# Three weight units taken together behind a norm, the third from a place of its own, in a two-block transformer kernel

## The chip, the cores and the metric

The kernel runs on one core of a Trainium2 chip. A time is the device microseconds of one execution, and the figure for the kernel is the median of its runs. One further execution was taken with the hardware profiler; its span, from the first instruction to the last, is what the rows below come from.

## The reference

The input is one sequence of 256 tokens of 1024 numbers. It goes through one mixer block with a feed-forward part, and then through two hybrid layers, each again with a feed-forward part. All of it is in float32. What matters here is the order of normalizations and matrix products:

```python
h = rms_norm(x, norm_mix_g[l]);  proj = h @ w_in[l]        # "win1"
...
x = x + merged @ w_out[l]                                  # "wout1"
h = rms_norm(x, norm_ffn_g[l])                             # norm "ffn"
u = causal_dwconv(h @ ffn_up[l], ...)                      # "up1"
x = x + (gelu(u_gate) * u_val) @ ffn_down[l]               # "down1"
x = rms_norm(x, final_norm_g)                              # norm "final"
# two layers, l = 0, 1:
proj = einsum('bsd,de->bse', x, w_in)                      # "win20", "win21"
...
x = layer_norm(ALPHA * x + mix, ln1_g, ln1_b)              # "wout2l", norm "ln1l"
up = causal_dwconv_2(einsum('bsd,df->bsf', x, w_up), ...)  # "up20", "up21"
x = layer_norm(ALPHA * x + ffn, ln2_g, ln2_b)              # "down2l", norm "ln2l"
```

Each norm needs sums over all 1024 numbers of a token, so nothing of the product behind it can start before the last tile in front of it is finished.

## The kernel before, in words

**Layout.** Numbers of a token lie on the partitions, tokens along the free dimension: x is eight tiles of 128x256 (KT = 8). Every weight matrix is cut into units of eight 128x128 blocks (seven in part of the down products). There are 400 units, in the order of `unit_table`; `START[name]` is the number of the first unit of a phase (up1 88, win20 156, up20 210, win21 278, up21 332).

**Precision.** Each operand is split into a high and a low part in a rounded float32 format, and each block product is three matmuls of 256 columns: high by high, high by low, low by high (`product_of`, lines 1097 to 1103). A unit of eight blocks is 24 matmuls into one PSUM bank. The unit's last matmul increments `unit_done`.

**The ring of three.** A unit goes through four steps on four queues, with three slots (RING = 3) of each of `raw`, `whi`, `wlo`; unit n has slot n % 3:

- SyncE issues the load into `raw` (`load`, L522). It waits until the low part of unit n - 3 is made (`split_lo`).
- ScalarE copies `raw` into `whi` (`hi_part`, L766). It waits for the load and until TensorE has done unit n - 3.
- VectorE subtracts: `wlo = raw - whi` (`lo_part`, L1400). It waits for `split_hi` of the unit.
- TensorE waits for `split_lo` of the unit (`begin`, line 1105).

So the split of unit n + 3 begins when unit n is finished, and runs beside units n + 1 and n + 2. In a phase, ScalarE first takes the result of unit n out of its bank (L1046, L1044 in up, L1079 in win2), and then makes the high part of unit n + 3; in up, VectorE does the two convolution taps of unit n (L1712, L1715) ahead of the low part.

**Behind a norm.** VectorE makes the normalized tiles (L1419 for an rms norm, L1440 for a layer norm), ScalarE their high parts (L810, L800), VectorE their low parts (L1404, L1444; two of eight on GpSimd after an rms norm, L702). TensorE follows tile by tile in `ramp` (lines 1125 to 1140): by `TOGETHER` it takes block k of the first two units of the phase as soon as normalized tile k is there, 6 matmuls for each k, 48 in all. The third unit follows by `plain`, and so do all others. Between the tiles in front of the norm and the ramp, TensorE does the sums over the partitions and small filler matmuls (`warm`, L1117).

**The third unit before.** Its `whi` slot is that of the last unit in front of the norm. Its high part is made on ScalarE behind the sums: after `norm_inverse` in an rms norm, between tiles 2 and 3 in a layer norm (`norm_shift`, line 794). Its low part is made on VectorE after all normalized tiles: in `up` by the body of i = 0, in win2 by a call ahead of the loop (line 1755).

Of the kernel before, what the change touches and what calls it, by code (L numbers as in the profile page):

```python
# [80 lines left out]
UNITS, START = unit_table()  # L81
FFNS = ("1", "20", "21")


# [120 lines left out]
def build(nc, args, out):  # L205
# [3 lines left out]
    with ctx:  # L209
# [63 lines left out]
        var_rows, mean_rows = fprod[:, 0, :], fprod[:, 2, :]  # L273
        shift_rows = acc[:, 0, :]
        pads = sb("pads", [P, 4, 2, 16 + S])
        zpad = sb("zpad", [P, 2, 2 + S])
# [77 lines left out]
        def repeat(eng, name, count, per, body, peel_first=False):  # L354

            rounds = count // per
            lo, hi = (1 if peel_first else 0), rounds - 1
            n0 = START[name]  # L360
            for i in range(lo * per):
                body(n0 + i, i, 0)
            if hi > lo:
                with eng.Fori(lo, hi) as it:
                    for i in range(per):
                        body(n0 + i, i, it)
            for i in range(hi * per, count):
                body(n0 + i, i, 0)

        def head(j):  # L370
# [75 lines left out]
        def bank_of(r):  # L446
            return unit_bank[r % 3]
# [310 lines left out]
        def _(act):  # L758
            def hi_part(n, it=0, per=0):
                if n >= len(UNITS):  # L760
                    return
                blocks = UNITS[n][3]

                wait(act, arrived[n % RING], 16 * (n // RING + 1), it, 16 * per // RING)
                wait(act, unit_done, n - RING + 1, it, per)
                act.activation(whi[:, n % RING, 0:blocks * P], raw[:, n % RING, 0:blocks * P], ACT.Copy).then_inc(split_hi, 1)  # L766

# [25 lines left out]

            def norm_shift(which, last, third=None):

                for t in range(KT):
                    if t == 3 and third is not None:
                        hi_part(third)
                    act.wait_ge(scaled, KT * LNI[which] + t + 1)
                    act.activation(x[:, t, :] if last else xhi[t], dev[:, t, :], ACT.Identity, bias=col(which[:3] + "_b" + which[3], t)) \  # L800
                        .then_inc(normed_act if last else x_hi, 1)
                    if t == 3 and which in NEXT:
                        shift_copy(NEXT[which])
# [197 lines left out]
            def wout(first, which, begun=0):  # L1001
                for t in range(KT):
                    if t >= begun:
                        hi_part(first + t + 2)
                    if t == 0:
                        load_log()
                    if t:
                        square(which, t - 1)
                square(which, KT - 1)

            def down(name, which):
                def body(n, i, it):
# [12 lines left out]
                repeat(act, name, DOWN, 6, body, peel_first=True)  # L1025
                if which not in LNI:
                    square(which, KT - 2)
                square(which, KT - 1)

# [30 lines left out]
            norm_inverse("ffn", RMS_EPS)  # L1060
            hi_part(START["up1"] + 2)
            norm_hi("ffn", dev)
            ffn(0, "up1", "ffn_1", False)
            down("down1", "final")
            norm_inverse("final", RMS_EPS)
            hi_part(START["win20"] + 2)
            norm_hi("final", x)

            for l in range(LAYERS2):
# [18 lines left out]
                norm_inverse(f"ln1{l}", LN_EPS)  # L1088
                norm_shift(f"ln1{l}", False, START[f"up2{l}"] + 2)
# [3 lines left out]
                norm_shift(f"ln2{l}", l == LAYERS2 - 1, START[f"win2{l + 1}"] + 2 if l < LAYERS2 - 1 else None)  # L1093


        @block.tensor
        def _(pe):
            def product_of(ps, slot, block, hi, lo, first, last):

                w = slice(block * P, (block + 1) * P)  # L1100
                pe.matmul(ps, whi[:, slot, w], hi, start=first, stop=False)  # L1101
                pe.matmul(ps, whi[:, slot, w], lo, start=False, stop=False)  # L1102
                return pe.matmul(ps, wlo[:, slot, w], hi, start=False, stop=last)  # L1103

# [16 lines left out]

            TOGETHER = [(u, k) for k in range(KT) for u in range(2)]
            LATER = [(u, k) for u in range(2) for k in range(5)] + TOGETHER[10:]

            def ramp(n, result, ready, order=TOGETHER, split=(xhi, xlo), shift=False):

                hi, lo = split
                met = [0, 0]
                for u, k in order:
                    if k == 0:  # L1130
                        begin(n + u, result + u)
                    if k == max(met):
                        pe.wait_ge(*ready[k])
                    met[u] = k + 1
                    mm = product_of(bank_of(result + u)[:, 0:S], (n + u) % RING, k, hi[k], lo[k], k == 0, k == KT - 1)
                    if k == KT - 1:
                        mm.then_inc(unit_done, 1)
                    if shift and (u, k) == (1, 0):
                        pe.matmul(shift_sum, ones_hi[:], hi[0], start=True, stop=True).then_inc(shift_ready, 1)

            def plain(n, result, ps, it=0, per=0, rper=0, ready=None, split=(xhi, xlo)):
                hi, lo = split
                begin(n, result, it, per, rper)
                for k in range(KT):
                    if ready is not None:
                        pe.wait_ge(*ready[k])
                    mm = product_of(ps, n % RING, k, hi[k], lo[k], k == 0, k == KT - 1)
                mm.then_inc(unit_done, 1)
# [146 lines left out]
            def merge_unit(n, r, t, parts, ready):  # L1295
# [6 lines left out]
                for which, (y, blocks) in enumerate(parts):  # L1302
                    ps = branch_bank(r, which, t)
                    for k in range(blocks):
                        mm = product_of(ps, n % RING, b, yhi[y + k], ylo[y + k], k == 0, k == blocks - 1)
                        b += 1
# [17 lines left out]
            def up(name, which):  # L1324
                def body(n, i, it):
                    r = RESULT[name] + i
                    if i < 2 and isinstance(it, int):
                        if i == 0:
                            ramp(n, r, lows(which), shift=which in NEXT)
                        return  # L1330
# [3 lines left out]
            def down(name, f, which):  # L1334
                def body(n, i, it):
# [5 lines left out]
                    if i in (2, 4) and isinstance(it, int) and it == 0:  # L1341
                        product_of(ps_turn[:, 0:S], n % RING, 0, xhi[0], xlo[0], True, True)
                    for k in range(DOWN_PARTS[part]):
                        mm = product_of(down_bank(name, t)[:, 0:S], n % RING, k, fhi[:, k0 + k, :], flo[:, k0 + k, :],
                                        k0 + k == 0, k0 + k == FT - 1)
# [20 lines left out]
            for l in range(LAYERS2):  # L1366
                name = f"win2{l}"
                ramp(START[name], RESULT[name], lows("ln20" if l else "final"), shift=True)
                for p, (kind, t) in enumerate(PLAN2):
                    n, r = START[name] + p, RESULT[name] + p  # L1370
                    if kind == "merge":
                        merge_unit(n, r, t, [(0, 2), (2, 4), (6, 2)],
                                   [(out_read, 8 + 4 * (l + 1)), (pool_lo, l + 1), (gconv_lo, 2 * l + 2)])
                    elif p > 1:
                        plain(n, r, bank_of(r)[:, 0:S])
# [9 lines left out]
        def _(dve):  # L1385
# [8 lines left out]
            def lo_part(n, it=0, per=0):  # L1394
                if n >= len(UNITS):
# [3 lines left out]
                wait(dve, split_hi, n + 1, it, per)  # L1399
                dve.tensor_tensor(wlo[:, n % RING, w], raw[:, n % RING, w], whi[:, n % RING, w].bitcast(f32), ALU.subtract) \  # L1400
                    .then_inc(split_lo, 1)
# [295 lines left out]
            def wout(name, which, alpha, begun=0):  # L1697
                for t in range(KT):
                    if t >= begun:
                        lo_part(START[name] + t + 2)  # L1700
                    if t == 0 and which in LNI:
                        dve.wait_ge(x_shifted, KT * (LNI[which] + 1))
                    residual(name, t, START[name] + t, alpha, bank_of(RESULT[name] + t), which)

            def up(f, name, cols, width):
                def body(n, i, it):
                    lo_part(n + 2, it, 6)
                    q = KT + UPT * f + i
# [10 lines left out]
            def down(name, which, alpha):  # L1719
                def body(n, i, it):  # L1720
# [11 lines left out]
                    if i % 3 == 2:  # L1732
                        residual(name, t, n, alpha, down_bank(name, t), which, it, 6, 2)
                repeat(dve, name, DOWN, 6, body, peel_first=True)

            for n in range(WIN1):
# [150 lines left out]
```

## Time and profile before

| | us |
|---|---|
| median of three runs | 1200.94 (1200.78 to 1202.69) |
| the profiled execution's own time | 1200.8 |
| its span | 1199.0 |
| TensorE busy in it | 1181.3 |
| VectorE busy | 849.5 |
| ScalarE busy | 713.8 |
| GpSimd busy | 441.5 |

The mean granted clock of TensorE is 0.998 of 2.4 GHz. A busy share of TensorE is counted from the modelled ends of pipelined matmuls: a matmul of 256 columns has a row of 0.28 us, and the next begins 0.11 to 0.12 us after it. A pause of TensorE shows therefore in the distance between the starts of matmuls rather than in its busy time. In the timeline a row is: start in us, duration in us, engine, line, operation, output<-inputs, sizes, how many in a row were merged, and in brackets how long the engine had been idle and what ended that.

### The profile page before, as it was taken

To read this page: it belongs to the slowest core of one execution; us is meant where nothing else is said; L and a number is where in the kernel's file an instruction comes from. 1 tells how busy PE (TensorE), PEld (TensorE's weight loads), DVE (VectorE), ACT (ScalarE), POOL (GpSimd) and SP (SyncE) were. 2 spreads that over 40 slices of the span, in tenths; PEclk is the share of its full clock that TensorE was granted. 3 is DMA by queue.
4 is the path that set the end of the run, shared out by engine and by line. 5 is a ranking of instruction groups with operands and counts; after the bars stand their busy time and mean duration, and the time that the engine had idled before them with its cause. 6 is when DMAs were issued, how large, how long until landed. Compare 5 with 4: busy or idle time off the path is not lost.

```text
span 1199.0 us, 27004 instructions
## 1 busy us (share of the span) xinstructions
PE 1181.3 (99%) x10128; PEld 1160.6 (97%) x10128; DVE 849.5 (71%) x1399; ACT 713.8 (60%) x1242; POOL 441.5 (37%) x415
## 2 busy tenths in 40 slices
PE   8999999999999999999999999999999999999997
PEld 7999999999999999999999999999999999999996
DVE  5868665676877764878667877755877677877754
ACT  5767667545766654566456666645566456666643
POOL 3007315123344402232338534423622349444422
PEclk9999999999999999999999999999999999999999
DMA  7554445654655666454554655566544554665563
GB/s 260 184 165 159 132 157 164 192 192 159 194 192 192 188 189 197 158 161 147 181 189 140 203 189 193 179 196 182 160 162 155 188 173 151 201 197 191 180 201 100
DMA packets 60286, 212.61 MB, mean 177 GB/s; under 512 B 6688, under 2 KB 7968, under 8 KB 60064
## 3 DMA queue, kind: packets, MB, share of 16 engines
q1 hardware_dynamic: 60192, 211.32, 55.9%
q8 instruction: 64, 1.05, 0.4%
q14 instruction: 30, 0.25, 0.1%
HBM read 210.24 MB, written 1.05 MB: 176 GB/s over the span
## 4 chain that ended last, share of the span: by engine, by line
PE 89%; DVE 5%; issue 2%; ACT 2%; POOL 1%; POOLq 0%; DVEq 0%; ACTq 0%
PE bank L1101 28%; PE bank L1103 28%; PE bank L1102 28%; DVE wlo L1400 2%; PE bank L1117 1%; PE bank L1249 1%; PE bank L1218 1%; ACT whi L766 1%; PE bank L1229 1%; PE bank L1273 1%; DVE prob L1565 1%; DVE prob L1540 0%; POOL u L683 0%; DVE u L1632 0%; PE bank L1158 0%
## 5 line engine op out<-in xcount | busy, mean ns | idle before, releaser
L1400 DVE TENSOR_TENSOR wlo<-raw,whi 128x1024 fp32r<-128x1024 f32 (+1 forms) x400 | 499.9, 1250 | 204.2 <-ACT whi L766 202.5
L1101 PE MATMUL bank<-shifted,whi 128*128 128x256 f32 x2296 | 639.0, 278 | 1.5 <-POOL shifted L702 1.1
L1102 PE MATMUL bank<-shifted,whi 128*128 128x256 f32 x2296 | 636.2, 277 | 0.0
L1103 PE MATMUL bank<-shifted,wlo 128*128 128x256 f32 x2296 | 635.8, 277 | 0.0
L766 ACT ACTIVATE whi<-raw 128x1024 fp32r<-128x1024 f32 (+1 forms) x400 | 416.5, 1042 | 149.4 <-PE bank L1103 137.9
L1101 PEld LDWEIGHTS bank<-shifted,whi 128*128 128x128 f32 x2296 | 431.6, 188 | 3.4 <-POOL shifted L702 1.3
L1103 PEld LDWEIGHTS bank<-shifted,wlo 128*128 128x128 f32 x2296 | 431.7, 188 | 0.0
L1102 PEld LDWEIGHTS bank<-shifted,whi 128*128 128x128 f32 x2296 | 431.1, 188 | 0.0
L662 POOL TENSOR_TENSOR fprod<-ugate,uval 128x256 f32<-128x256 f32 x66 | 95.5, 1447 | 197.5 <-DVE uval L1715 188.2
L1101 PE MATMUL bank<-fhi,whi 128*128 128x256 f32 x528 | 145.8, 276 | 0.0
L1102 PE MATMUL bank<-flo,whi 128*128 128x256 f32 x528 | 145.7, 276 | 0.0
L1103 PE MATMUL bank<-fhi,wlo 128*128 128x256 f32 x528 | 145.7, 276 | 0.0
L1101 PE MATMUL bank<-aligned,whi 128*128 128x256 f32 x334 | 101.7, 305 | 3.4 <-DVE aligned L1404 3.4
L683 POOL TENSOR_TENSOR u<-u,tmp 128x256 f32<-128x256 f32 x48 | 53.4, 1112 | 134.2 <-DVE tmp L1674 132.2
L1101 PEld LDWEIGHTS bank<-fhi,whi 128*128 128x128 f32 x528 | 99.1, 188 | 0.0
L1102 PEld LDWEIGHTS bank<-flo,whi 128*128 128x128 f32 x528 | 99.1, 188 | 0.0
L1103 PEld LDWEIGHTS bank<-fhi,wlo 128*128 128x128 f32 x528 | 99.1, 188 | 0.0
L1103 PE MATMUL bank<-aligned,wlo 128*128 128x256 f32 x334 | 93.2, 279 | 0.0
L1102 PE MATMUL bank<-aligned,whi 128*128 128x256 f32 x334 | 92.3, 276 | 0.0
L1101 PEld LDWEIGHTS bank<-aligned,whi 128*128 128x128 f32 x334 | 62.8, 188 | 12.0 <-issue 9.1
L696 POOL TENSOR_TENSOR acc<-acc,dev 128x256 f32<-128x256 f32 x34 | 36.4, 1069 | 82.9 <-DVE dev L1694 51.8
L1102 PEld LDWEIGHTS bank<-aligned,whi 128*128 128x128 f32 x334 | 62.9, 188 | 0.4
(218 smaller groups left out, 1258.7 us busy)
## 6 DMA issues: line engine op xcount, KB each, us to landing
raw<-in_w_win SPq DMA_DIRECT2D x140, 512.0 KB, 3.5
raw<-in_w_up SPq DMA_DIRECT2D x132, 512.0 KB, 3.5
raw<-in_w_down SPq DMA_DIRECT2D x48, 448.0 KB, 3.5
raw<-in_w_merge SPq DMA_DIRECT2D x32, 512.0 KB, 3.6
raw<-in_w_out SPq DMA_DIRECT2D x24, 512.0 KB, 4.3
raw<-in_w_down SPq DMA_DIRECT2D x24, 512.0 KB, 3.5
x<-in_x SPq DMA_DIRECT2D x4, 256.0 KB, 4.5
rgw<-in_rg_w SPq DMA_DIRECT2D x1, 1024.0 KB, 10.1
```

What stands on the lines that cost most here:

```text
L662: pool.tensor_tensor(tile(fprod, t % 3), tile(ugate, t % 3), tile(uval, t % 3), ALU.mult).then_inc(product, 1)
L683: ins = pool.tensor_tensor(m, m, branch_part(base, t, branch), ALU.add)
L696: pool.tensor_tensor(acc[:, sums, :], acc[:, sums, :], one, ALU.add).then_inc(done, 1)
L766: act.activation(whi[:, n % RING, 0:blocks * P], raw[:, n % RING, 0:blocks * P], ACT.Copy).then_inc(split_hi, 1)
L1101: pe.matmul(ps, whi[:, slot, w], hi, start=first, stop=False)
L1102: pe.matmul(ps, whi[:, slot, w], lo, start=False, stop=False)
L1103: return pe.matmul(ps, wlo[:, slot, w], hi, start=False, stop=last)
L1117: pe.matmul(bank_of(result)[:, S:S + P], ones[:], ones[:], start=True, stop=True)
L1218: mm = pe.matmul(score_bank(j)[:, rows:rows + across], u[qp:qp + HD, q, rows:cols], u[kp:kp + HD, k, 0:across], start=True, stop=True, ski ...
L1229: mm = pe.transpose(ps_turn[:, i * P:(i + 1) * P], prob[:, s, i * P:(i + 1) * P], ident)
L1249: mm = pe.matmul(ps_out[m * i:m * i + m, half * P:S], v[:, half, c:c + m], probT[:, job % 2, half * S:half * P + S], start=half == 0, stop ...
L1400: dve.tensor_tensor(wlo[:, n % RING, w], raw[:, n % RING, w], whi[:, n % RING, w].bitcast(f32), ALU.subtract) \
```

## The change

The third unit of the five phases up1, win20, up20, win21 and up21 (units 90, 158, 212, 280, 334) gets a place of its own for its high and low part, `third`. The place lies where `pads` and `zpad` lie, which only the win2 phases use, at other times. Its high part no longer waits for the last unit in front of the norm, but for the one before that; ScalarE makes it ahead of the last square in front of the sums, and VectorE makes its low part right after the last residual. The parts made behind the sums go. TensorE takes the three units together by the order `THREE`: for k = 0, 1, 2 blocks of the first two units; for k = 3 to 7 block k of the first two and block k - 3 of the third; then blocks 5, 6, 7 of the third. The first unit then ends with matmul 57 of 72 (before: 45), the second with matmul 60 (before: 48), the third with matmul 72 (before: 72). The waits of all other units are as they were.

```diff
+THIRD = [START[name] + 2 for name in ("up1", "win20", "up20", "win21", "up21")]
...
+        with ExitStack() as three:
+            sb("line_third", [P, 16], stack=three)
+            third = sb("third", [P, 2, 8 * P], r32, stack=three)
         pads = sb("pads", [P, 4, 2, 16 + S])
...
+        def high_part(n, it=0):
+            return third[:, 0, :] if n in THIRD and isinstance(it, int) else whi[:, n % RING, :]
+        def low_part_of(n, it=0):
+            return third[:, 1, :] if n in THIRD and isinstance(it, int) else wlo[:, n % RING, :]
...
                 wait(act, arrived[n % RING], 16 * (n // RING + 1), it, 16 * per // RING)
-                wait(act, unit_done, n - RING + 1, it, per)
-                act.activation(whi[:, n % RING, 0:blocks * P], raw[:, n % RING, 0:blocks * P], ACT.Copy).then_inc(split_hi, 1)
+                wait(act, unit_done, n - RING + (0 if n in THIRD and isinstance(it, int) else 1), it, per)
+                act.activation(high_part(n, it)[:, 0:blocks * P], raw[:, n % RING, 0:blocks * P], ACT.Copy).then_inc(split_hi, 1)
...
-            def norm_shift(which, last, third=None):
+            def norm_shift(which, last):
                 for t in range(KT):
-                    if t == 3 and third is not None:
-                        hi_part(third)
...
             def wout(first, which, begun=0):
...
                         square(which, t - 1)
+                hi_part(first + KT + 2)
                 square(which, KT - 1)
             def down(name, which):
...
                     square(which, KT - 2)
+                hi_part(START[name] + DOWN + 2)
                 square(which, KT - 1)
...
             norm_inverse("ffn", RMS_EPS)
-            hi_part(START["up1"] + 2)
...
             norm_inverse("final", RMS_EPS)
-            hi_part(START["win20"] + 2)
...
             TOGETHER = [(u, k) for k in range(KT) for u in range(2)]
+            THREE = [(u, k - 3 * (u == 2)) for k in range(KT + 3) for u in range(3) if 0 <= k - 3 * (u == 2) < KT]
...
-                met = [0, 0]
+                met = [0, 0, 0]
...
-                    if i < 2 and isinstance(it, int):
+                    if i < 3 and isinstance(it, int):
                         if i == 0:
-                            ramp(n, r, lows(which), shift=which in NEXT)
+                            ramp(n, r, lows(which), THREE, shift=which in NEXT)
...
-                ramp(START[name], RESULT[name], lows("ln20" if l else "final"), shift=True)
+                ramp(START[name], RESULT[name], lows("ln20" if l else "final"), THREE, shift=True)
...
-                    elif p > 1:
+                    elif p > 2:
                         plain(n, r, bank_of(r)[:, 0:S])
...
                     residual(name, t, START[name] + t, alpha, bank_of(RESULT[name] + t), which)
+                lo_part(START[name] + KT + 2)
             def up(f, name, cols, width):
                 def body(n, i, it):
-                    lo_part(n + 2, it, 6)
+                    if i or not isinstance(it, int):
+                        lo_part(n + 2, it, 6)
...
                 repeat(dve, name, DOWN, 6, body, peel_first=True)
+                lo_part(START[name] + DOWN + 2)
...
-                lo_part(START[f"win2{l}"] + 2)
```

The products read their weight parts through `high_part` and `low_part_of` in place of the slot.

## Rows read from the trace of the kernel before

**Rows 1.** Page: busy us, share of the span, instructions; shares of the chain by engine

```profile
PE 1181.3 (99%) x10128; PEld 1160.6 (97%) x10128; DVE 849.5 (71%) x1399; ACT 713.8 (60%) x1242; POOL 441.5 (37%) x415
...
PE 89%; DVE 5%; issue 2%; ACT 2%; POOL 1%; POOLq 0%; DVEq 0%; ACTq 0%
```

**Rows 2.** Timeline, TensorE behind the first FFN norm: start us, us, engine line op

```profile
297.68 0.32 PE L1101 MATMUL bank<-shifted,whi 128*128 128x256 f32 x1
...
300.89 0.28 PE L1101 MATMUL bank<-shifted,whi 128*128 128x256 f32 x1
...
304.00 0.31 PE L1101 MATMUL bank<-aligned,whi 128*128 128x256 f32 x1
```

**Rows 3.** Timeline, ScalarE and VectorE in the same stretch (engine columns as above)

```profile
299.48 1.21 DVE L1400 TENSOR_TENSOR wlo<-raw,whi 128x1024 fp32r<-128x1024 f32 x1
...
301.10 0.56 ACT L1046 ACTIVATE ugate<-bank,vec 128x256 f32<-128x256 f32 x1 [2.31 <-PE bank L1103]
...
301.56 1.05 ACT L766 ACTIVATE whi<-raw 128x1024 fp32r<-128x1024 f32 x1
...
302.21 0.48 DVE L1715 SCALAR_TENSOR_TENSOR ugate<-bank,vec,ugate 128x254 f32<-128x254 f32 x1
...
302.65 1.23 DVE L1400 TENSOR_TENSOR wlo<-raw,whi 128x1024 fp32r<-128x1024 f32 x1
```

**Rows 4.** Timeline, TensorE, ScalarE, VectorE behind the norm into up20

```profile
652.70 0.36 PE L1101 MATMUL bank<-shifted,whi 128*128 128x256 f32 x1
...
656.35 0.47 ACT L1044 ACTIVATE ugate<-bank,vec 128x256 f32<-128x256 f32 x1 [2.00 <-PE bank L1103]
...
657.28 0.28 PE L1101 MATMUL bank<-shifted,whi 128*128 128x256 f32 x1
...
657.80 1.23 DVE L1400 TENSOR_TENSOR wlo<-raw,whi 128x1024 fp32r<-128x1024 f32 x1
...
659.32 0.28 PE L1101 MATMUL bank<-aligned,whi 128*128 128x256 f32 x1
```

**Rows 5.** Timeline, TensorE and ScalarE behind the norm into win20

```profile
484.03 0.28 PE L1101 MATMUL bank<-shifted,whi 128*128 128x256 f32 x1
...
487.41 0.39 ACT L1079 ACTIVATE u<-bank 128x256 f32<-128x256 f32 x1 [2.42 <-PE bank L1103]
...
490.39 0.28 PE L1101 MATMUL bank<-aligned,whi 128*128 128x256 f32 x1
```

**Rows 6.** Timeline, VectorE alone in that stretch

```profile
488.77 1.23 DVE L1400 TENSOR_TENSOR wlo<-raw,whi 128x1024 fp32r<-128x1024 f32 x1 [1.89 <-ACT whi L766]
```

**Rows 7.** Timeline, TensorE and ScalarE behind the norm into win21

```profile
840.14 0.38 PE L1101 MATMUL bank<-shifted,whi 128*128 128x256 f32 x1
...
843.77 0.38 ACT L1079 ACTIVATE u<-bank 128x256 f32<-128x256 f32 x1 [1.97 <-PE bank L1103]
...
846.85 0.28 PE L1101 MATMUL bank<-aligned,whi 128*128 128x256 f32 x1
```

**Rows 8.** Timeline, VectorE alone in that stretch

```profile
845.13 1.23 DVE L1400 TENSOR_TENSOR wlo<-raw,whi 128x1024 fp32r<-128x1024 f32 x1 [1.28 <-ACT whi L766]
```

**Rows 9.** Timeline, around the sums of the first FFN norm

```profile
291.53 0.42 ACT L987 ACTIVATE dev<-x 128x256 f32<-128x256 f32 x1 [1.77 <-DVE x L1694]
...
293.57 1.04 ACT L766 ACTIVATE whi<-raw 128x1024 fp32r<-128x1024 f32 x1
293.67 1.26 DVE L1419 SCALAR_TENSOR_TENSOR dev<-x,vec,bank 128x256 f32<-128x256 f32 x3 [2.17 <-ACT bank L781]
```

**Rows 10.** Timeline, around the sums of the norm into win20

```profile
471.82 3.29 SPq L522 DMA_DIRECT2D raw<-in_w_win  x2
...
477.59 0.42 ACT L987 ACTIVATE dev<-x 128x256 f32<-128x256 f32 x1 [1.41 <-DVE x L1694]
```

**Rows 11.** Timeline, VectorE at the sums of the norm into win21

```profile
834.22 0.42 DVE L1428 TENSOR_TENSOR fprod<-bank,fprod 128x256 f32<-128x256 f32 x1 [1.38 <-PE bank L1187]
```

**Rows 12.** Page: DMA issues, KB each, median us from issue to landing

```profile
raw<-in_w_win SPq DMA_DIRECT2D x140, 512.0 KB, 3.5
```

More of the change, by code:

```diff
@@ L1088, in _ @@
                 norm_inverse(f"ln1{l}", LN_EPS)
-                norm_shift(f"ln1{l}", False, START[f"up2{l}"] + 2)
+                norm_shift(f"ln1{l}", False)
                 ffn(1 + l, f"up2{l}", f"ffn_2{l}", True)
@@ L1092, in _, with product_of @@
                 norm_inverse(f"ln2{l}", LN_EPS)
-                norm_shift(f"ln2{l}", l == LAYERS2 - 1, START[f"win2{l + 1}"] + 2 if l < LAYERS2 - 1 else None)
+                norm_shift(f"ln2{l}", l == LAYERS2 - 1)
         @block.tensor
         def _(pe):
-            def product_of(ps, slot, block, hi, lo, first, last):
+            def product_of(ps, n, it, block, hi, lo, first, last):
                 w = slice(block * P, (block + 1) * P)
-                pe.matmul(ps, whi[:, slot, w], hi, start=first, stop=False)
-                pe.matmul(ps, whi[:, slot, w], lo, start=False, stop=False)
-                return pe.matmul(ps, wlo[:, slot, w], hi, start=False, stop=last)
+                pe.matmul(ps, high_part(n, it)[:, w], hi, start=first, stop=False)
+                pe.matmul(ps, high_part(n, it)[:, w], lo, start=False, stop=False)
+                return pe.matmul(ps, low_part_of(n, it)[:, w], hi, start=False, stop=last)
             def begin(n, result, it=0, per=0, rper=0, banks=3):
@@ L1134, in ramp @@
                     met[u] = k + 1
-                    mm = product_of(bank_of(result + u)[:, 0:S], (n + u) % RING, k, hi[k], lo[k], k == 0, k == KT - 1)
+                    mm = product_of(bank_of(result + u)[:, 0:S], n + u, 0, k, hi[k], lo[k], k == 0, k == KT - 1)
                     if k == KT - 1:
@@ L1146, in plain @@
                         pe.wait_ge(*ready[k])
-                    mm = product_of(ps, n % RING, k, hi[k], lo[k], k == 0, k == KT - 1)
+                    mm = product_of(ps, n, it, k, hi[k], lo[k], k == 0, k == KT - 1)
                 mm.then_inc(unit_done, 1)
@@ L1304, in merge_unit @@
                     for k in range(blocks):
-                        mm = product_of(ps, n % RING, b, yhi[y + k], ylo[y + k], k == 0, k == blocks - 1)
+                        mm = product_of(ps, n, 0, b, yhi[y + k], ylo[y + k], k == 0, k == blocks - 1)
                         b += 1
@@ L1341, in body @@
                     if i in (2, 4) and isinstance(it, int) and it == 0:
-                        product_of(ps_turn[:, 0:S], n % RING, 0, xhi[0], xlo[0], True, True)
+                        product_of(ps_turn[:, 0:S], n, it, 0, xhi[0], xlo[0], True, True)
                     for k in range(DOWN_PARTS[part]):
-                        mm = product_of(down_bank(name, t)[:, 0:S], n % RING, k, fhi[:, k0 + k, :], flo[:, k0 + k, :],
+                        mm = product_of(down_bank(name, t)[:, 0:S], n, it, k, fhi[:, k0 + k, :], flo[:, k0 + k, :],
                                         k0 + k == 0, k0 + k == FT - 1)
@@ L1399, in lo_part @@
                 wait(dve, split_hi, n + 1, it, per)
-                dve.tensor_tensor(wlo[:, n % RING, w], raw[:, n % RING, w], whi[:, n % RING, w].bitcast(f32), ALU.subtract) \
+                dve.tensor_tensor(low_part_of(n, it)[:, w], raw[:, n % RING, w], high_part(n, it)[:, w].bitcast(f32), ALU.subtract) \
                     .then_inc(split_lo, 1)
```

## The prediction

> **What bounds the kernel now.** I read the page first, for the engine that sets the time. TensorE is busy 99% of the span, and the chain of work that ended last lies on it for 89% [rows 1]. So what counts is when TensorE starts each matmul, and a pause of TensorE is lost unless a later pause swallows it. Then I read the timeline behind the five norms that the change touches, and in it the starts of TensorE's matmuls, counted from the first matmul of the ramp (number 0).
>
> Behind the first FFN norm, matmul 18 starts at 297.68, matmul 45 at 300.89, and matmul 72, the first of unit 91, at 304.00 [rows 2]. The 54 matmuls from 18 to 72 take 6.32 us, 0.117 each. Behind the norm into win20 the same 54 take 6.36 us, 0.1178 each [rows 5]. These two are rms norms, and their ramps hold no pause to speak of. Behind the norm into up20, a layer norm, the 54 take 6.62 us, while the last 18 of them (from matmul 54 at 657.28) take 2.04, 0.1133 each [rows 4]. At that pitch 54 would take 6.12, so 0.50 us of pauses lie there: TensorE waits a little for each normalized tile. Into win21 the 54 take 6.71 us [rows 7]; at 0.1178 they would take 6.36, so 0.35 us of pauses. The norm into up21 repeats up20's pattern.
>
> The second thing to see is how the ring is refilled behind the ramp. Unit 91 has the slot of unit 88, and its split starts when unit 88, the first of the ramp, is done. Matmul 44 is unit 88's last. ScalarE takes its result at 301.10, which is 0.21 after matmul 45 has started [rows 2, 3]. It then makes the high part of unit 91 from 301.56. VectorE does two taps, the second at 302.21, and the low part from 302.65 to 303.88 [rows 3]. From ScalarE's start to the end of the low part are 2.78 us. TensorE starts unit 91 at 304.00, 0.12 later [rows 2]. With 0.21 and 0.12 the refill takes 3.11 us from the start of matmul 45, and the 27 matmuls from 45 to 72 take 304.00 - 300.89 = 3.11 us. Unit 91 comes just in time; **there is no slack in this refill**. In up20 the middle part is 656.35 to 659.03, 2.68 us [rows 4]. In the win2 phases, which have no taps, it is 2.59 us: 487.41 to 490.00 [rows 5, 6] and 843.77 to 846.36 [rows 7, 8].
>
> **The change part by part.**
>
> *The order of the ramp.* By the new order unit 88 ends with matmul 57 in place of 45, since the third unit's matmuls are put between. From the start of its successor, matmul 57, only 15 matmuls are left to matmul 72, not 27. The split of the fourth unit still waits for the first one: its wait is not touched, as only the third has a place of its own. So the refill, some 3 us, has 15 x 0.117 = 1.76 us to hide behind. What is queued behind TensorE's wait for the fourth unit's low part is everything that TensorE has left.
>
> I work it out forward from matmul 18, which is the same in both: up to there both orders have the same matmuls. From there TensorE has 9 matmuls for each tile, about 1.03 us, in place of 6, about 0.69. A pause at a tile of at most 0.50/5 us or so goes away by that, so I take the undisturbed pitch. The fourth unit starts at (matmul 18) + 39 x pitch + 0.21 + middle part + 0.12:
>
> - up1: 297.68 + 39 x 0.117 + 0.21 + 2.78 + 0.12 = 305.35, before 304.00: +1.35.
> - win20: 484.03 + 39 x 0.1178 + 0.21 + 2.59 + 0.12 = 491.54, before 490.39: +1.15.
> - up20: 652.70 + 39 x 0.1133 + 0.21 + 2.68 + 0.12 = 660.13, before 659.32: +0.81.
> - win21: 840.14 + 39 x 0.1178 + 0.21 + 2.59 + 0.12 = 847.65, before 846.85: +0.80.
> - up21, as up20: +0.81.
>
> The sum is **+4.92 us**. The layer norms' smaller terms already contain the pauses that the third unit fills. With every pitch at 0.1133 it is 4.92 - 39 x (0.0037 + 2 x 0.0045) = 4.4; with every pitch at 0.1178, 4.92 + 39 x (0.0008 + 2 x 0.0045) = 5.3. The units after the fourth have room again: in up1 the next low part was made about 2 us after this one, and a unit takes 24 x 0.1133 = 2.7 us.
>
> *The high part, moved ahead of the sums.* 1.06 us or so on ScalarE, five times (1.04 us where it stood) [rows 9]. It stands ahead of the last square, which feeds the sums. ScalarE was idle for 1.77 us there in up1 and 1.41 into win20 [rows 9, 10], waiting for TensorE's last tile, so it fits with 0.35 to 0.7 us over, if its load has landed. Into win20 the load was issued at 471.82, as soon as the low part of unit 155 was made, and takes 3.5 us in the median [rows 10, 12], so it lands at about 475.3; ScalarE has until 477.59 - 1.06 = 476.5. I cost it at nothing. If that cover is gone, each us of delay is a us in front of the norm.
>
> *The low part, moved ahead of the norm.* 1.23 us on VectorE, behind the last residual. VectorE's idle time there was 2.17 in up1 and, least of all, 1.38 us into win21 [rows 9, 11]: hidden, by 0.15 us in the tightest place. Behind it are queued the first norm operations. Nothing.
>
> *What goes behind the sums.* The high part at 293.57 delayed the first high part of a normalized tile a little in the rms norms, but VectorE does three scalings first, until 293.67 + 1.26 [rows 9], and reaches the first low part only then. I bound the gain by 0 and 0.1 us in each of two norms and take 0. The low part at 299.48 [rows 3] ran beside the ramp and cost nothing; its going gives nothing.
>
> *The queues of SyncE and GpSimd.* The load that reuses the third unit's `raw` slot waits for its low part, which is now made some 8 us earlier: before at 299.48 [rows 3], now behind the last residual, about when the last square starts at 291.53 [rows 9]. The load goes out earlier; later ones still wait for the splits. GpSimd does nothing for weight parts. Nothing on the path. The place `third` shares its memory with `pads`, with no wait added.
>
> **Sum.** The profiled execution took 1200.8 us (span 1199.0, 1.8 around it), the median 1200.94, so the difference is 0.1. 1200.94 + 4.9 = 1205.8 us.
>
> **Rivals.**
>
> *The third unit fills pauses and nothing is lost* (the other side). TensorE pauses in each layer-norm ramp, and with a third unit ready it need not. The Trainium skill, page Perfetto Trace Analysis, section Optimization Strategy, reads consistent bubbles on the engine that should be saturated as a possible sign that there isn't enough SBUF for the next tile; by that rule another place should shorten the time. The trace agrees that there are bubbles, but they end with the normalized tile and not with a weight part. From rows the gain is 0.50 + 0.35 + 0.50 = 1.35 us, with 0.1 to 0.2 from the rms norms: 1199.4 us. It decides if the refill, from the first unit's end to the fourth unit's low part, takes less than the 15 matmuls, 1.76 us. Against it: the refill took 2.9 to 3.1 us in all four places that I read, and in up1 unit 91 started 0.12 us after its low part ended. Chance 0.04.
>
> *The lost time is swallowed, or the order does not do what it says.* If TensorE waited later for VectorE in the win2 phases whatever it did before, the two win2 terms would go: 4.92 - 1.95 = 2.97, 1203.9 us. I hold this for the forecast's lower end, since VectorE's work there starts from TensorE's results. If the third unit is in truth taken after the first two, all stays: 1200.9 us. Chance of that, or of all five terms being swallowed, 0.05.
>
> *The moved split lands on the sums as well.* If loads land late, or VectorE's low part grows past its 1.38 us in the tight places, the norm starts later on top of the forecast. At most 1.06 us each time, five times, if no cover held: up to 1205.8 + 5.3 = 1211.1 us; half of it, about 1208.5, is likelier. For it speaks only the tightness in two places. Chance 0.08.
>
> **How the numbers follow.** The forecast has the remaining 0.83, and its own range is 1203.9 (win2 terms swallowed) to 1207.0 (highest pitch, and some tenths for the tight places). The chance outside is 0.17, so the range need not reach to the rivals: 1203.9 to 1207.2. Slower by over 0.2% (over 2.4 us, about what a measurement of this kernel can tell from no change) takes the forecast and the third rival, 0.91; within 0.2% 0.05; faster, from the first rival, which with 1.5 us would partly fall within, 0.04.
>
> **What would show it right or wrong.** Right: behind each of the five norms TensorE starts its ramp when it did, has no pause between matmuls 18 and 72, and then pauses 1.2 to 1.4 us before matmul 72's successor unit, with VectorE's low part (L1400 of before) as what ends the wait; the high part of the fourth unit starts about 0.6 us after matmul 57 has. ScalarE's last square and the first scaling stand where they stood against the last matmul in front of the norm. Wrong: no pause at the fourth unit (then the refill found more cover than I count), or an idle gap of TensorE ahead of the ramp that has grown (then the moved split is not hidden), or later pauses of TensorE in win2 that have shrunk by as much.

## The result and the profile after

The changed kernel takes 1206.81 us in the median of 6 runs (1205.35 to 1208.06), the kernel before 1201.45 in 6 runs of the same comparison (1200.78 to 1202.69). The ratio is 1.0042, with a 95% interval of 1.0032 to 1.0052: the change makes the kernel 5.4 us slower, and the time lies 1 us above the forecast, inside the range.

The profiled execution took 1208.06 us, 7.3 more than that of before, and 2.5 of these lie in the first phase, win1, whose code is the same in all nine traces: it takes 210.8 to 210.9 us in five of them and 212.9 to 213.5 in four, this one among them, with a granted clock of 0.50 to 0.54 between 16 and 22 us where the five have 1.00; I therefore compare the other phases from here on, and leave out of the figures below one execution of the kernel "both together" that took 1944.07 us at a mean granted clock of 0.567.

The page of the changed kernel, the rows that answer to [rows 1]:

```profile
span 1206.3 us, 27004 instructions
PE 1183.9 (98%) x10128; PEld 1162.3 (96%) x10128; DVE 847.8 (70%) x1399; ACT 714.9 (59%) x1242; POOL 433.0 (36%) x415
PE 88%; DVE 6%; issue 2%; ACT 2%; POOL 1%; POOLq 0%; DVEq 0%; ACTq 0%
```

TensorE is still what bounds the kernel. The view of TensorE's waits says what is new: what it waited for, us in total, times, longest. First the two largest rows of the kernel before, then the two largest of the changed one:

```profile
PE bank L1101 <- DVE aligned L1404: 3.4, 3, 1.8
PE bank L1117 <- ACT ones_hi L816: 2.5, 1, 2.5
```

```profile
PE bank L1112 <- DVE wlo L1412: 5.1, 5, 1.2
PE bank L1112 <- DVE aligned L1416: 3.2, 3, 1.8
```

Before, no row named a low part. Now five waits, one behind each of the five norms, cost 5.1 us together. (The view counts a wait from the modelled end of the row in front, which is 0.17 us later than the start that the next matmul would have had at the usual distance; by the starts the five waits are 6.0 us.) This is the first of them in the timeline, behind the first FFN norm (start, length, engine; idle time and its releaser in brackets). It answers to [rows 2, 3]:

```profile
299.88 0.31 PE L1112 MATMUL bank<-shifted,whi 128*128 128x256 f32 x1
...
304.36 0.28 PE L1112 MATMUL bank<-shifted,whi 128*128 128x256 f32 x1
...
304.56 0.56 ACT L1059 ACTIVATE ugate<-bank,vec 128x256 f32<-128x256 f32 x1 [3.58 <-PE bank L1114]
...
305.02 1.05 ACT L779 ACTIVATE whi<-raw 128x1024 fp32r<-128x1024 f32 x1
...
305.68 0.48 DVE L1729 SCALAR_TENSOR_TENSOR ugate<-bank,vec,ugate 128x254 f32<-128x254 f32 x1
...
305.95 0.28 PE L1114 MATMUL bank<-shifted,third 128*128 128x256 f32 x1
...
306.11 1.23 DVE L1412 TENSOR_TENSOR wlo<-raw,whi 128x1024 fp32r<-128x1024 f32 x1
...
307.39 0.39 PE L1112 MATMUL bank<-aligned,whi 128*128 128x256 f32 x1 [1.17 <-DVE wlo L1412]
...
307.61 0.28 PE L1113 MATMUL bank<-aligned,whi 128*128 128x256 f32 x1
```

The rows are matmuls 18, 57, 71, 72 and 73 with the refill between them. Matmul 57 follows the first unit's last. ScalarE takes that unit's result 0.20 us later, splits off the high part of the fourth unit at 305.02, VectorE finishes the low part at 307.34, and TensorE goes on at 307.39: 3.03 us, of which only the matmuls 57 to 71, until about 306.06, lie beside it. Compare [rows 2]: the same refill lay beside 27 matmuls, and nothing stood still. The other four waits:

```profile
494.93 0.39 PE L1112 MATMUL bank<-aligned,whi 128*128 128x256 f32 x1 [0.91 <-DVE wlo L1412]
...
664.60 0.39 PE L1112 MATMUL bank<-aligned,whi 128*128 128x256 f32 x1 [1.07 <-DVE wlo L1412]
...
852.94 0.38 PE L1112 MATMUL bank<-aligned,whi 128*128 128x256 f32 x1 [0.98 <-DVE wlo L1412]
...
1022.98 0.39 PE L1112 MATMUL bank<-aligned,whi 128*128 128x256 f32 x1 [1.01 <-DVE wlo L1412]
```

The five phases behind the norms (up1, win20, up20, win21, up21, each from its first matmul to that of the next phase) take 650.54 us, 5.25 more than the 645.29 of before. The two rms ramps start 0.11 us earlier each, which shortens wout1 and down1. The remaining phases agree within 0.1 us. Net, that is 5.03 us.

The moved splits are seen around the sums, in front of the first FFN norm, the rows that answer to [rows 9]:

```profile
292.05 1.06 ACT L779 ACTIVATE third<-raw 128x1024 fp32r<-128x1024 f32 x1
...
293.72 1.22 DVE L1412 TENSOR_TENSOR third<-raw,third 128x1024 fp32r<-128x1024 f32 x1
...
293.83 0.42 ACT L998 ACTIVATE dev<-x 128x256 f32<-128x256 f32 x1 [0.72 <-DVE x L1706]
...
295.97 1.26 DVE L1431 SCALAR_TENSOR_TENSOR dev<-x,vec,bank 128x256 f32<-128x256 f32 x3 [1.03 <-ACT bank L794]
```

ScalarE's idle time ahead of the last square fell from 1.77 to 0.72 us, and VectorE's ahead of the first scaling from 2.17 to 1.03. Both splits went into idle time, with something left over.

### The profile page after: what moved, and what is told of

Read it like the earlier page. It is cut to its first block, busy times and chain, and to the rows that moved or that the text cites. A ratio compares the mean times of both kernels' runs of the same rounds, so it can differ in the third digit from the quotient of the medians.

```text
span 1206.3 us, 27004 instructions
## 1 busy us (share of the span) xinstructions
PE 1183.9 (98%) x10128; PEld 1162.3 (96%) x10128; DVE 847.8 (70%) x1399; ACT 714.9 (59%) x1242; POOL 433.0 (36%) x415
## 4 chain that ended last, share of the span: by engine, by line
PE 88%; DVE 6%; issue 2%; ACT 2%; POOL 1%; POOLq 0%; DVEq 0%; ACTq 0%
PE bank L1112 28%; PE bank L1114 27%; PE bank L1113 27%; DVE wlo L1412 2%; PE bank L1128 1%; PE bank L1261 1%; PE bank L1230 1%; ACT whi L779 1%; PE bank L1241 1%; PE bank L1285 1%; DVE prob L1577 1%; DVE prob L1552 0%; POOL u L696 0%; DVE u L1644 0%; PE bank L1170 0%
## 5 line engine op out<-in xcount | busy, mean ns | idle before, releaser
L1412 DVE TENSOR_TENSOR wlo<-raw,whi 128x1024 fp32r<-128x1024 f32 (+1 forms) x395 | 492.0, 1247 | 213.1 <-ACT whi L779 211.2
L1112 PE MATMUL bank<-shifted,whi 128*128 128x256 f32 x2261 | 629.7, 279 | 1.3 <-POOL shifted L715 0.9
L1113 PE MATMUL bank<-shifted,whi 128*128 128x256 f32 x2261 | 627.5, 278 | 0.0
L1114 PE MATMUL bank<-shifted,wlo 128*128 128x256 f32 x2261 | 627.2, 277 | 0.0
L779 ACT ACTIVATE whi<-raw 128x1024 fp32r<-128x1024 f32 (+1 forms) x395 | 411.5, 1042 | 151.6 <-PE bank L1114 135.6
L1112 PEld LDWEIGHTS bank<-shifted,whi 128*128 128x128 f32 x2261 | 426.0, 188 | 2.9 <-POOL shifted L715 1.2
L1114 PEld LDWEIGHTS bank<-shifted,wlo 128*128 128x128 f32 x2261 | 426.2, 189 | 0.0
L1113 PEld LDWEIGHTS bank<-shifted,whi 128*128 128x128 f32 x2261 | 425.5, 188 | 0.0
```

The costliest lines, as they stand in the source:

```text
L779: act.activation(high_part(n, it)[:, 0:blocks * P], raw[:, n % RING, 0:blocks * P], ACT.Copy).then_inc(split_hi, 1)
L1112: pe.matmul(ps, high_part(n, it)[:, w], hi, start=first, stop=False)
L1113: pe.matmul(ps, high_part(n, it)[:, w], lo, start=False, stop=False)
L1114: return pe.matmul(ps, low_part_of(n, it)[:, w], hi, start=False, stop=last)
L1412: dve.tensor_tensor(low_part_of(n, it)[:, w], raw[:, n % RING, w], high_part(n, it)[:, w].bitcast(f32), ALU.subtract) \
```

## The experiments

Two theories at the start. **The order** costs the time: the first unit ends at matmul 57, the refill of its slot has 15 matmuls to hide behind, and TensorE waits for the rest. The rival: **the moved splits or the own place** cost it, by what they delay at the sums or on VectorE. Each kernel is the changed one with the edit shown. The times are medians, each beside the kernel before on the same chip: 1202.32 us (27 runs) for the kernels lag and four, 1202.18 (23 runs) for first, first_four and filled.

### The lag of the third unit: 8, 5 and 0 tiles

The third unit follows the first two by 3 normalized tiles in the change. One number sets it:

```diff
-THREE = [(u, k - 3 * (u == 2)) for k in range(KT + 3) for u in range(3) if 0 <= k - 3 * (u == 2) < KT]
+THREE = [(u, k - 8 * (u == 2)) for k in range(KT + 8) for u in range(3) if 0 <= k - 8 * (u == 2) < KT]
```

and the same with 5 and with 0. With 8 the third unit comes behind the first two, as before the change, while its place and the moved splits stay. The first unit's successor is then matmul 45, with a lag of 5 it is 51, with 3 it is 57, with 0 it is 66.

Lag 8:

> The changed kernel with the third unit's 24 matmuls moved behind the other two units (a lag of 8 tiles in place of 3). Its own place and the moved splits stay. Theory 1 (the refill of the fourth unit lies open because the first unit ends 12 matmuls later): the first unit ends with matmul 45 again, 27 matmuls cover the refill of 2.8 to 3.0 us, no wait for a low part behind any ramp, the small pauses of the layer-norm ramps come back; time 1200.5 to 1201.5 us, the kernel before's. Rival (the splits moved ahead of the sums, or the new place, cost the time): stays at 1205 us or more.

Measured: 1202.0 us (11 runs), ratio 0.9998 (0.9989 to 1.0007). Lag 5:

> The changed kernel with a lag of 5 tiles in place of 3. The first unit ends with matmul 51, so 21 matmuls (2.4 us) are left for the refill of 2.8 to 3.0 us. Theory 1: a wait of 0.3 to 0.6 us behind each of the five ramps, in all +2.0 us against the kernel before, 1203 us. Rival (the interleaving as such, or the moved splits, cost the time): as the change, 1205.5 us.

Measured: 1203.51 us (11 runs), ratio 1.0021 (1.0012 to 1.0030). Lag 0:

> The changed kernel with no lag: the three units side by side from the first tile. The first unit ends with matmul 66, 6 matmuls (0.7 us) are left. Theory 1: a wait of about 2.2 us behind each ramp, 1 us more than in the change, partly paid back in the layer-norm ramps where the third unit fills two more small pauses; in all +9.5 us against the kernel before, 1210.5 us. Rival (interleaving as such): 1205 to 1206 us. Rival (the third unit fills pauses): faster than the change.

Measured: 1214.89 us (4 runs), ratio 1.0115 (1.0099 to 1.0131). TensorE's waits for the low part, in lag 5 first, then in lag 0; lag 8 has no such row:

```profile
PE bank L1112 <- DVE wlo L1412: 1.8, 5, 0.5
```

```profile
PE bank L1112 <- DVE wlo L1412: 10.4, 5, 2.2
```

The distance from matmul 71 to 72, from the timelines (0.11 us is no wait):

| lag | matmuls left | up1 | win20 | up20 | win21 | up21 | five phases against before |
|---|---|---|---|---|---|---|---|
| 8 | 27 | 0.11 | 0.11 | 0.11 | 0.11 | 0.11 | -0.90 |
| 5 | 21 | 0.76 | 0.48 | 0.67 | 0.62 | 0.67 | +2.85 |
| 3 (the change) | 15 | 1.44 | 1.19 | 1.35 | 1.26 | 1.29 | +5.25 |
| 0 | 6 | 2.46 | 2.27 | 2.37 | 2.35 | 2.37 | +12.62 |

From lag 5 to 3, six matmuls go from behind the first unit to ahead of its end, 6 x 0.1136 = 0.68 us; the wait grows by 0.62 to 0.71. From 3 to 0 nine go, 1.02 us; it grows by 1.02 to 1.09. **The wait is the refill less the matmuls left, and the order is the whole loss.** The rival is out: lag 8 has the own place and both moved splits, and loses nothing.

Lag 0 lost 12.6 us against the kernel before where I had forecast 9.5, and not by its waits. (Its 1214.89 us is 4.4 above the 1210.5 of the forecast; the other 1.3 is the kernel before, at 1202.32 here.) In the profiled execution, TensorE's granted clock fell behind two of the five waits, in up1 and win21. This is the table by stretch in up1 (us, busy time and instructions of PE, PEld, DVE, ACT and POOL, granted clock, DMA share, GB/s): in front of the wait, around it, the first matmuls of the fourth unit, the rest of that unit, and the next one. The last two rows are the rest of the fourth unit in win21, and the whole fourth unit in up20, where the clock stayed.

```profile
303.00:306.00 3.00, 3.00 (x29) 3.00 (x27) 0.00 (x0) 0.45 (x1) 0.00 (x0) 1.00 0.00 0
306.00:308.38 2.38, 0.20 (x3) 0.00 (x1) 2.19 (x4) 2.38 (x4) 0.00 (x0) 1.00 0.00 0
308.38:309.40 1.02, 1.02 (x8) 1.02 (x9) 0.98 (x3) 1.00 (x2) 0.00 (x0) 0.96 0.00 0
309.40:312.60 3.20, 3.20 (x17) 3.20 (x16) 2.85 (x4) 2.49 (x5) 0.73 (x1) 0.50 0.82 224
312.83:316.00 3.17, 3.17 (x29) 3.17 (x28) 2.16 (x4) 1.96 (x4) 1.01 (x1) 1.00 0.68 238
...
859.20:862.40 3.20, 3.20 (x17) 3.20 (x16) 2.52 (x6) 0.04 (x1) 0.47 (x1) 0.52 0.84 274
...
668.89:671.80 2.91, 2.91 (x24) 2.91 (x25) 2.71 (x5) 2.89 (x4) 0.75 (x1) 1.00 0.56 173
```

For 3.2 us the clock is 0.50, the 1.2 GHz level, and only 17 records fit where 29 fit into the 3.17 us behind. The matmuls 73 to 95 take 4.09 us there and 4.12 in win21, against 2.51 and 2.52 before, so the low clock costs 3.2 us in the two places. In the other three they take 2.52 to 2.59. The rest of the sum: 11.3 us of waits at matmul 72, 0.5 by a longer distance from matmul 72 to 73 (last section), less 2.6 us by which the matmuls 0 to 71 are shorter than before, for the most part since the pauses for the normalized tiles are filled; with the clock 12.4, of the 12.62 measured.

### A place of its own for the fourth unit

If the refill is what is late, a further place, for the fourth unit, should take the wait away with the order kept. Its split is made behind the normalized tiles, into memory of the attention's `prob` that is free there:

```diff
+FOURTH = [n + 1 for n in THIRD]
...
+            fourth = sb("fourth", [P, 2, 8 * P], r32, stack=four)
...
-                wait(act, unit_done, n - RING + (0 if n in THIRD and isinstance(it, int) else 1), it, per)
+                wait(act, unit_done, n - RING + (0 if n in THIRD and isinstance(it, int) else -1 if n in FOURTH and isinstance(it, int) else 1), it, per)
...
+            hi_part(START["up1"] + 3)
...
+            lo_part(START["up1"] + 3)
```

and likewise at the other four norms; the splits that stood in the loops are left out there.

> The changed kernel, order of lag 3, with a place of its own for the fourth unit's weight parts as well (on the attention tiles, unused there), its split made behind the normalized tiles while the ramp runs, so that it no longer waits for the first unit. Theory 1: the wait for the fourth unit's low part behind the five ramps goes; what is late next is the first unit's bank in the up phases, by 0 to 0.2 us each; the pauses of the layer-norm ramps stay filled; time 1199.2 to 1199.8 us, faster than the kernel before by 1.1 to 1.7 us. Rival (interleaving, the banks or the place of the third unit cost the time): 1204 us or more.

Measured: 1202.48 us (11 runs), ratio 1.0006 (0.9997 to 1.0015). The wait for the low part is gone, and with it 5.0 us of the five phases against the change (645.52). But nothing is won against before, where I had forecast 1.1 to 1.7 us: the rival is out, and the size of the gain was wrong, since the next thing is late. The timeline of this kernel in up1, the matmuls 71 and 72 and what stands between:

```profile
303.54 0.48 DVE L1742 SCALAR_TENSOR_TENSOR ugate<-bank,vec,ugate 128x254 f32<-128x254 f32 x1
...
303.81 0.28 PE L1127 MATMUL bank<-shifted,third 128*128 128x256 f32 x1
...
304.17 0.35 PE L1125 MATMUL bank<-aligned,fourth 128*128 128x256 f32 x1
```

The weight parts lie ready, yet matmul 72 starts 0.36 us behind matmul 71, and 0.15 behind the end of VectorE's second tap at 304.02: the fourth unit writes into the first unit's bank, and VectorE still reads it there. That happens in the up phases alone (0.36, 0.26 and 0.27 us; 0.11 and 0.12 in win20 and win21, which have no taps). Besides, the matmuls of the fourth unit run at a distance of 0.119 us in all five places, where they had 0.114 before, which the forecast did not have. I come back to that.

### An order in which the first unit leads

The theory says that the third unit may be used as a filler as long as the first one still ends early. So the third takes a tile only where TensorE would wait, and the first unit's last tiles go ahead of the second's:

```diff
-THREE = [(u, k - 3 * (u == 2)) for k in range(KT + 3) for u in range(3) if 0 <= k - 3 * (u == 2) < KT]
+FIRST_LN = [(0, 0), (1, 0), (2, 0), (0, 1), (1, 1), (0, 2), (1, 2), (2, 1), (0, 3), (1, 3), (0, 4), (1, 4), (0, 5), (1, 5), (0, 6), (0, 7), (1, 6), (1, 7)] + [(2, k) for k in range(2, KT)]
+FIRST_RMS = TOGETHER[:13] + [(0, 7), (1, 6), (1, 7)] + [(2, k) for k in range(KT)]
...
-                            ramp(n, r, lows(which), THREE, shift=which in NEXT)
+                            ramp(n, r, lows(which), FIRST_LN if which in LNI else FIRST_RMS, shift=which in NEXT)
```

and likewise in the win2 phases. The first unit's successor is matmul 48 behind the layer norms (24 left) and 42 behind the rms norms (30 left).

> The changed kernel with another order of the ramp, no new place: the first unit always goes ahead, and the third only fills the pauses. Behind a layer norm the first unit ends with matmul 48 (two blocks of the third are put between), behind an rms norm with matmul 42 (none); then the rest of the second and the third. Theory 1 (what counts is how many matmuls are left behind the first unit for a refill of 2.85 to 3.0 us): 24 matmuls are 2.75 us, so a wait of 0.1 to 0.3 us behind a layer norm and none behind an rms norm; pauses of 0.35 to 0.5 us in the layer-norm ramps filled; 0.7 to 1.7 us less than the kernel before, no more than 1200.3 us where that takes 1201. Rival (third unit's blocks between the others cost by themselves): 1 us or more above the run with lag 8.

Measured: 1201.25 us (12 runs), ratio 0.9991 (0.9982 to 1.0000). The five phases take 643.98 us, 1.31 less than before and 6.6 less than with the changed order. Behind the layer norms the 24 matmuls are not quite enough, as these two rows of up20, matmuls 71 and 72, show:

```profile
658.22 0.28 PE L1114 MATMUL bank<-shifted,third 128*128 128x256 f32 x1
...
658.54 0.39 PE L1112 MATMUL bank<-aligned,whi 128*128 128x256 f32 x1
```

They are 0.32 us apart, a wait of 0.21; it is the same in win21 and up21, and behind the rms norms there is none. The rival is out: the time is not above that of lag 8. Whether it lies below is not shown. The interval reaches 1.0000, lag 8's five phases were already 0.90 us shorter than before, and the distance between matmuls alone can move a ramp by 0.25 us: one and the same order takes 8.56 us from matmul 0 to 71 in win20 of the change, at 0.1179 us a matmul, and 8.31 in the kernel "filled" below, at 0.1138.

### Both together

> The order of the run first, and the fourth unit's own place and early split as in the run four. In the run four the wait for the low part was gone, but in the up phases TensorE waited 0.25 us for the first unit's bank (second tap ends, 0.14 us later the matmul), and its matmuls then kept a longer distance for some units. With the first unit ended at matmul 48 or 42 the bank is free in time: no wait behind the ramps, pauses filled. Theory 1: 2.0 to 2.9 us less than the kernel before, 0.17 to 0.24%. Rival (the distance of the matmuls grows with the fourth unit's place, not with the pause): equal to the run four, within 0.5 us of the kernel before.

The edit is the two above in one kernel. Measured: 1200.86 us in the median of 11 runs, ratio 0.9990 (0.9981 to 0.9999). The five phases take 643.42 us, 1.87 less than before. All five ramps run from matmul 0 to 72 in 8.35 to 8.43 us, with no wait at the end; before they took 8.48 to 9.18. Its median is the lowest of the study, but it can't be told from the order alone (0.9991), and the gain against before is hardly above what is measurable. The gain is 1.3 us by the medians, less than the 2.0 to 2.9 that I had forecast, and what the rival named is there without any pause at matmul 72: again the fourth unit's matmuls have a distance of 0.119 us, 2.74 us from matmul 72 to 95 in place of 2.63 to 2.66, and the fifth unit's in the up phases 0.118 in place of 0.114: from matmul 72 to 240 that gives back 0.8 us in the five places.

### Does the pause cause the longer distance?

In the changed kernel, too, the fourth unit takes longer than before (2.73 to 2.82 us from matmul 72 to 95). To see whether TensorE's pause brings that about, four small products of ones are put in front of the fourth unit:

```diff
+            def fill():
+                for _ in range(4):
+                    pe.matmul(ps_turn[:, S:S + P], ones[:], ones[:], start=True, stop=True)
...
+                    if i == 3 and isinstance(it, int):
+                        fill()
```

> The changed kernel as it is (lag 3), with four small float32 matmuls on ones, about 1 us, put on TensorE ahead of the fourth unit in each of the five phases, while it waits for the low part; their result is not used. They take no time from the wait. If the longer distance of matmuls behind the wait (the fourth unit took 2.85 to 3.0 us in place of 2.74 to 2.9) comes of the pause, it goes: 0.1 us less in each phase, 0.5 us below the change. If it comes of something else, the time is the change's. In neither case does the loss of 4.9 us go.

Measured: 1206.52 us (5 runs), ratio 1.0044 (1.0031 to 1.0057), the same as the change. The wait for the low part in this kernel's view of TensorE's waits fell as it had to:

```profile
PE bank L1112 <- DVE wlo L1421: 0.6, 3, 0.3
```

but matmul 72 starts as late as before (1.25 to 1.44 us behind 71), and the fourth unit stays at 2.74 to 2.81 us from matmul 72 to 95. Work in the pause gives nothing back. These rows of win20 are the four products (taken together, until 492.45) and the matmuls 72 and 73:

```profile
491.40 1.05 PE L1133 MATMUL bank<-ones 128*128 128x128 f32 x8
...
492.54 0.38 PE L1112 MATMUL bank<-aligned,whi 128*128 128x256 f32 x1
...
492.76 0.28 PE L1113 MATMUL bank<-aligned,whi 128*128 128x256 f32 x1
```

TensorE stood still for 0.1 us here, and yet matmul 73 starts 0.22 us behind matmul 72, as in the change. So standing still for long is not what makes that distance long. Why some units run at 0.118 or 0.119 throughout is not settled by this run.

## Why the prediction was right

**The fourth unit's start.** The step that decided was to see that the refill starts with the first unit's end and takes some 3 us, whatever TensorE does meanwhile. That it had no slack before holds strictly in up1 alone: there unit 91 started 0.12 us after its low part was made, in win20, up20 and win21 the low part was ready 0.39, 0.29 and 0.49 us ahead [rows 4, 5, 6, 7, 8]. The sum adds up the parts from matmul 18 on and so takes that into account. Between matmuls 18 and 72 the prediction has +1.35, +1.15, +0.81, +0.80 and +0.81 us, 4.92 together; measured are +1.19, +1.08, +0.85, +0.70 and +1.04, 4.86 together. In up1 the parts were as said: 0.20 from matmul 57 to ScalarE's start (said 0.21), 2.78 for the middle part (2.78), and 0.05 to the next matmul (0.12). The high part starts 0.66 us behind matmul 57 (0.6). The pauses at matmul 72 are 1.08 to 1.33 us above the usual distance (said: 1.2 to 1.4).

That the sum is so close is in part luck. The refill from matmul 57 to 72 was 0.07 to 0.08 us shorter than said in each place, 0.4 together, and the 39 matmuls in front of it took 0.3 us more together: 4.48 us in up1 in place of 4.56, but 4.54 in up20 and 4.70 in up21 in place of 4.42. In up20 the pauses did not go at once (matmul 19 starts 0.20 us behind 18). In up21 there is one such pause too, but above all the matmuls from 24 to 71 follow at 0.118 us without one, where the forecast had 0.1133. Which of these distances a ramp gets could not be read from the kernel before: win20 has 0.1179 in the change, as was forecast, and 0.1138 in "filled" with the same order.

**What was missing.** The fourth unit itself was taken at its old length. It took 0.59 us more in the five places (+0.17, +0.09, +0.12, +0.10 and +0.11), of which 0.5 is the longer distance from matmul 72 to 73 (see the last section). With it the sum would have been 5.5, and the phases show 5.25.

**The rms norms' gain** was bounded by 0 and 0.1 us in each and taken as 0. It is 0.11 in each, at the upper end: the ramps start so much earlier, with and without the new order (lag 8 has it too).

**The moved splits** cost nothing, as said. Into win20, ScalarE's place without much room, it kept 0.46 us where 0.35 was forecast; into win21, VectorE's tightest place, 0.24 us were left where 0.15 was forecast, as this row of the timeline shows that answers to [rows 11]:

```profile
839.62 0.42 DVE L1440 TENSOR_TENSOR fprod<-bank,fprod 128x256 f32<-128x256 f32 x1 [0.24 <-PE bank L1199]
```

Lag 8 shows it in the time.

**The units behind the fourth** have room again: the waits of the changed kernel for a low part are five, one for each ramp.

**The rivals.** That the third unit fills pauses and nothing is lost was half right. The matmuls 0 to 71 got shorter by 0.13, 0, 0.41, 0.46 and 0.18 us, 1.18 together, where the rival had 1.35, but the refill took 3 us and not the 1.76 from which it decides, and the waits took five times as much, 6.0 us. The Trainium skill, page Perfetto Trace Analysis, section Optimization Strategy, reads consistent bubbles as a possible lack of SBUF. The runs don't show a gain from the one place more: with the old order the ratio is 0.9998, with the changed order 1.0042, and with the first unit kept in the lead 0.9991, whose interval reaches 1.0000; only with a second place on top, 0.9990, does the interval end below, at 0.9999. That the lost time is swallowed later: win20 and win21 lose 1.01 and 0.80 us over the whole phase, so it isn't. That the moved split lands on the sums: lag 8 would have shown it, and doesn't.

The forecast of 1205.8 us is 1.0 below the measured 1206.81. The kernel before was itself 0.5 us slower in the comparison than the median from which the sum started; against it the loss is 5.36 us, where 4.9 was forecast. In the traces it is 5.03: 4.86 at matmul 72 and 0.59 in the fourth unit, less 0.22 behind the rms norms and 0.2 spread over the rest of the five phases.

## What to carry to other kernels

When units of work share a ring of buffers, the order in which they are interleaved decides when the first buffer comes free. Count the instructions that are left behind the first unit's last, multiply by their distance, and set that against the refill; interleaving one more unit moves the first unit's end back by all that is put in front of it. A further buffer for the unit that comes last in a group can fill pauses, but only if the order still frees the first buffer in time, so let the first unit lead and use the others as fillers. Here even that was worth about 0.1%, at the edge of what could be measured; what the runs show beyond doubt is the loss when the first unit does not lead.

## What the runs showed of the hardware

**A wait costs 0.1 us on top of itself.** Behind each wait of TensorE for a low part the second matmul starts 0.22 to 0.23 us after the first, and not 0.12 (0.15 in up1 of before), in the change, lag 5 and lag 0 alike; the rows of matmuls 72 and 73 of up1 above are one such pair, 307.39 and 307.61. Where nothing is waited for, as in lag 8 in win20, up20, win21 and up21, it is 0.12. With five waits that is 0.5 us on top of the waits. In these runs it doesn't depend on the length of the wait: it is the same 0.22 to 0.23 behind 0.2 us (the order in which the first unit leads, layer norms), behind 2.2 us (lag 0), and behind some 0.1 us of standing still (win20 of "filled").

**The clock can fall behind a wait of some 2.2 us.** In the profiled execution of lag 0, two of five such waits were followed by 3.2 us at the 1.2 GHz level, beginning about 1 us after TensorE had started again; the other three, of much the same length, were not (2.46 and 2.35 us from matmul 71 to 72 where the clock fell, 2.27, 2.37 and 2.37 where it did not). Behind the waits of 0.9 to 1.2 us in the changed kernel the granted clock was 1.00 in all five places. What decides between the two was not tried.

**The distance between matmuls has more than one value at the full clock.** Most units run at 0.114 us, some at 0.118 or 0.119, and the ramp of win20 with the changed order at 0.1179 in one trace and 0.1138 in another. The fourth unit behind the ramp runs at 0.119 in all five places of the two kernels that give it a place of its own, and the units after it come back to 0.118, 0.115 and 0.114, with a granted clock of 1.00 and no wait. Whether the memory of that place, the earlier split or the work beside it does this was not tried and stays open.
